# A hybrid encoder step on one core: the dense weight units in three places of a pair, each loaded where its remainder will be

## What is computed

```
xn  = rmsnorm(x);  z = xn @ w_in            # 1024 x 10248
br0 = (heads of an mLSTM over z) @ w_br_mlstm
br1 = (gated, spatially mixed z) @ w_br_gmlp
br2 = (attention of z into 256 memory tokens, k = mn @ w_mem_k, v = mn @ w_mem_v) @ w_br_mem
x   = x + (sum_b sigmoid(gate_b) * br_b) @ w_out
x   = x + hier_moe(rmsnorm(x))              # top-1 of 4 groups, top-2 of 8 experts in it
y   = rmsnorm_final(x)
```

## Time and profile before

| | us |
|---|---|
| median of 3 runs | 952.02 (951.14 to 954.7) |
| profiled execution, its own time | 952.92 |
| its span | 951.2 |
| PE busy | 883.6 (93%) |
| DVE busy | 608.0 (64%) |
| ACT busy | 473.1 (50%) |
| SP's queue moved | 171.46 MB of 182.92 MB in all |

### The profile page before, as it was taken

One profiled execution on the slowest core, in us unless ns is written; L12 is line 12 of the kernel. 1 busy time (PEld: TensorE's weight loads), 2 busy tenths in 40 slices (PEclk: granted clock), 3 DMA queues, 4 the chain that ended last, 5 costly groups with the idle time before them and its releaser, 6 DMA issues.

```text
span 951.2 us, 13084 instructions
## 1 busy us (share of the span) xinstructions
PE 883.6 (93%) x5274; PEld 788.7 (83%) x5274; DVE 608.0 (64%) x816; ACT 473.1 (50%) x572; POOL 46.2 (5%) x107
## 2 busy tenths in 40 slices
PE   2989999989999999989999999689999999999993
PEld 2958998979988999989999989478877777887871
DVE  4545367773244455476656545757888889898974
ACT  3554355553333134253333334656767767667652
POOL 5001101100010111000000000000000000000000
PEclk9999999999999999999999999779999999999996
DMA  8624642333446657735444465018999999999941
GB/s 256 186 90 133 221 144 90 111 101 111 136 116 96 132 148 111 171 96 185 135 133 134 155 203 218 0 33 320 352 347 361 350 336 348 350 345 354 350 176 58
DMA packets 99203, 182.92 MB, mean 192 GB/s; under 512 B 5368, under 2 KB 71120, under 8 KB 99136
## 3 DMA queue, kind: packets, MB, share of 16 engines
q1 hardware_dynamic: 95232, 171.46, 55.5%
q0 software_dynamic: 3072, 8.37, 3.5%
q10 hardware_dynamic: 832, 2.18, 0.9%
HBM read 176.17 MB, written 5.82 MB: 191 GB/s over the span
## 4 chain that ended last, share of the span: by engine, by line
PE 58%; DVE 7%; DMA 7%; ACT 3%; issue 3%; DVEq 0%; SPq 0%; ACTq 0%
PE pj L519 28%; PE pj L767 14%; PE pj L789 8%; DMA arena<-in_w_in 4%; DMA arena<-in_w_exp_down 3%; ACT unit_r L861 1%; PE ms L803 1%; DVE unit_r L1161 1%; ACT w_r L865 1%; PE ms L732 1%; DVE w_r L1170 1%; PE ms L652 1%; PE pj L732 1%; PE ms L777 1%; PE ms L676 1%
## 5 line engine op out<-in xcount | busy, mean ns | idle before, releaser
L1161 DVE TENSOR_TENSOR unit_r<-arena,unit_r 128x2048 fp32r<-128x2048 f32 x64 | 146.7, 2292 | 199.2 <-ACT unit_r L861 194.0
L1170 DVE TENSOR_TENSOR w_r<-arena,w_r 128x2048 fp32r<-128x2048 f32 x96 | 218.5, 2288 | 42.4 <-ACT w_r L865 41.7
L519 PE MATMUL pj<-xn_r,unit_r 128*128 128x320 f32 x1536 | 237.4, 314 | 3.4 <-DVE unit_r L1161 3.4
L519 PEld LDWEIGHTS pj<-xn_r,unit_r 128*128 128x128 f32 x1536 | 228.6, 190 | 7.9 <-issue 3.5
L865 ACT ACTIVATE w_r<-arena 128x2048 fp32r<-128x2048 f32 x96 | 183.4, 1916 | 39.5 <-DMA arena<-in_w_exp_up 26.9
L767 PE MATMUL pj<-w_r,xg 128*128 128x512 f32 x768 | 190.9, 398 | 0.0
L767 PEld LDWEIGHTS pj<-w_r,xg 128*128 128x128 f32 x768 | 141.9, 189 | 30.6
L861 ACT ACTIVATE unit_r<-arena 128x2048 fp32r<-128x2048 f32 x64 | 121.9, 1905 | 45.7 <-PE pj L519 22.8
L789 PE MATMUL pj<-w_r,hidT 128*128 128x512 f32 x384 | 93.2, 391 | 2.7 <-DVE w_r L1170 1.5
L789 PEld LDWEIGHTS pj<-w_r,hidT 128*128 128x128 f32 x384 | 71.6, 188 | 20.1 <-DVE w_r L1170 3.8
L519 PE MATMUL pj<-unit_r,xn_r 128*128 128x256 f32 (+1 forms) x576 | 70.0, 282 | 1.6 <-DVE unit_r L1161 1.6
(11 more groups left out here) (315 smaller groups left out, 741.6 us busy)
## 6 DMA issues: line engine op xcount, KB each, us to landing
arena<-in_w_in SPq DMA_DIRECT2D x40, 1024.0 KB, 5.2
arena<-in_w_exp_gate SPq DMA_DIRECT2D x64, 512.0 KB, 4.4
arena<-in_w_exp_up SPq DMA_DIRECT2D x64, 512.0 KB, 5.5
arena<-in_w_exp_down SPq DMA_DIRECT2D x64, 512.0 KB, 5.1
arena<-in_w_mem_k SPq DMA_DIRECT2D x4, 1024.0 KB, 9.4
arena<-in_w_mem_v SPq DMA_DIRECT2D x4, 1024.0 KB, 5.2
arena<-in_w_br_mem SPq DMA_DIRECT2D x4, 1024.0 KB, 7.9
arena<-in_w_br_mlstm SPq DMA_DIRECT2D x4, 1024.0 KB, 5.0
```

What stands on the lines that cost most here:

```text
L519: last = mm(bank_of(s)[0:out_rows, 0:out_cols], l, r, start=k == 0, stop=k == len(pairs) - 1)
L1161: v.tensor_tensor(unit_r[n % RING][:, 1, :], ringw[:, n % RING, :], unit_r[n % RING][:, 0, :], ALU.subtract).then_inc(u_lo, 1)
L1170: v.tensor_tensor(w_r[u % NS][:, 1, :], raw_w[u % NS], w_r[u % NS][:, 0, :], ALU.subtract).then_inc(m_lo, 1)
```

## The change

The six blocks of 2048 values become three places of a pair. A raw unit lands in the second half of its place. ACT writes the high part to the first half and DVE the remainder over the raw unit. Load n waits until PE has left unit n-3, instead of for the remainder of n-2. ACT's wait for PE ahead of a high part goes, because the load's own wait now covers it. The positions of both splits in the programs stay where they were, behind the last step of unit n-2 (the constant 2 instead of RING). As RING is 3, unit 2 is loaded ahead of x. The load of expert unit 4 waits until PE has left unit 62, the last one in the place that it overwrites.

```diff
-RING = 2
+RING = 3
...
-        RING0 = region(RING * UW)
-        ringw = at(RING0, RING, UW)
+        RING0 = region(2 * UW)
         SP0 = region(2 * 2 * UW)
-        unit_r = [rounded(f"unit_r{k}", SP0 + k * 2 * UW, 2, UW) for k in range(2)]
+        UNIT_AT = [(SP0, SP0 + 2 * UW, RING0)[(k - len(UNITS) + 1) % RING] for k in range(RING)]
+        unit_r = [rounded(f"unit_r{k}", o, 2, UW) for k, o in enumerate(UNIT_AT)]
+        ringw = [at(o + UW, UW) for o in UNIT_AT]
...
                 if n >= RING:
-                    sp.wait_ge(u_lo, n - RING + 1)
+                    sp.wait_ge(ready["pj"], _last_use[n - RING] + 1)
...
                     elif u == 4:
-                        sp.wait_ge(u_lo, len(UNITS))
+                        sp.wait_ge(ready["pj"], _last_use[len(UNITS) - 2] + 1)
...
             def unit_first_part(n):
                 act.wait_ge(unit_full[n % RING], 16 * (n // RING + 1))
-                if n >= RING:
-                    act.wait_ge(ready["pj"], _last_use[n - RING] + 1)
-                af(unit_r[n % RING][:, 0, :], ringw[:, n % RING, :], ACT.Copy).then_inc(u_hi, 1)
+                af(unit_r[n % RING][:, 0, :], ringw[n % RING], ACT.Copy).then_inc(u_hi, 1)
...
-                if s["ring"] == "pj" and s["last"] and s["unit"] + RING < len(UNITS):
-                    unit_first_part(s["unit"] + RING)
+                if s["ring"] == "pj" and s["last"] and s["unit"] + 2 < len(UNITS):
+                    unit_first_part(s["unit"] + 2)
...
-                v.tensor_tensor(unit_r[n % RING][:, 1, :], ringw[:, n % RING, :], unit_r[n % RING][:, 0, :], ALU.subtract).then_inc(u_lo, 1)
+                v.tensor_tensor(unit_r[n % RING][:, 1, :], ringw[n % RING], unit_r[n % RING][:, 0, :], ALU.subtract).then_inc(u_lo, 1)
...
-                if s["ring"] == "pj" and s["last"] and s["unit"] + RING < len(UNITS):
-                    unit_second_part(s["unit"] + RING)
+                if s["ring"] == "pj" and s["last"] and s["unit"] + 2 < len(UNITS):
+                    unit_second_part(s["unit"] + 2)
```

More of the change, by code:

```diff
@@ L466, in _ @@
                 if n >= RING:
-                    sp.wait_ge(u_lo, n - RING + 1)
+                    sp.wait_ge(ready["pj"], _last_use[n - RING] + 1)
                 src = I[name][0, :, col:col + 256].rearrange("(k p) n -> p k n", p=128)
-                sp.dma_start(ringw[:, n % RING, :].rearrange("p (k n) -> p k n", n=256), src).then_inc(unit_full[n % RING], 16)
+                sp.dma_start(ringw[n % RING].rearrange("p (k n) -> p k n", n=256), src).then_inc(unit_full[n % RING], 16)
             def load_unit(lv, u):
```

## The result

The changed kernel took 982.74 us (median of 4 runs, 977.43 to 985.99) where the kernel before took 953.36 beside it (951.14 to 955.05): a ratio of 1.0304, interval 1.0252 to 1.0357, 29.4 us more. On another chip, later, it was 972.98 against 947.18: 1.0284, interval 1.0224 to 1.0344.

A forecast was written before the change was run, and what follows sets the result against it. PE was taken as the bound, busy 883.6 us of 951.2. Costs of 3.6 + 2.0 + 2.4 + 2.8 = 10.8 took the profiled 952.92 to 963.7, less 0.9 to the runs' median: 962.8, range 950 to 972.

The forecast's parts named there:

- terms 1 and 3: Unit 29's load caught in the slow stretch, cost 3.6 us; expert burst delayed behind load 63, cost 2.4 us.
- (c): Rival: every landing moves with its issue and unit 29 lands like unit 30; 20.5 us more, 972.5; chance 0.12.
- the four terms: Costs at unit 29 (3.6 us), other caught loads (2.0), handover to the experts (2.4) and the clock (2.8).
- Start: Unit 2's load goes ahead of x, so x lands later; cost 0, at most 5.2 us if cover is gone.
- Unit 29: Out of memory attention: load issued behind state outputs lands at 302, deadline 298.35; cost 3.6 us, bounds 0 and 6.9.
- The other loads: Units 39, 32 and 36, near later state outputs: +1 us for 39, +1 for both others; bounds -6.4 and 11.4.
- Unit 39: Slowest load, starting 5.4 us later: cost 5.4, 0 or a gain depending on what sets its landing; +1 us taken.
- (b): Rival: load 39 lands earlier, PE's 5.0 us of remainder waits and one clock loss vanish; 949.4; chance 0.08.
- Handover: Dense stage to experts: load 63 and the expert burst behind it start 6.8 us later; cost 2.4 us, bounds 0 and 3.5.
- Clock: Half clock behind new idle times at unit 29 and the handover, 1.4 us each; cost 2.8 us, bounds 0 and 2.8.
- rest of the handover, experts: Expert unit 4 asked for at about 592 instead of 586, read after the gather at 639; cost 0.
- signs: ACT idle before unit 29, unit 39 landing at 396 plus PE's lateness, expert wait about 7 us, half clock for 3.4 us.

The follow-up runs named there:

- c1: The changed kernel with only the prompt's n output per head, the sample's left out (half the small writes): 949.46 us, ratio 1.0017.
- a2: The changed kernel without the outputs of the state n (eight DMAs of 256 single 4-byte values): 950.48 us, ratio 1.0032.
- a3: The changed kernel without the outputs of the state C (eight DMAs of 256 KB), n outputs kept: 977.05 us, ratio 1.0306.
- b3: The changed kernel, complete, with n transposed on PE and written by two DMAs in rows of 512 bytes: 950.18 us, ratio 1.0044.
- c2: The changed kernel, complete, each head's n outputs held until the high part of unit 29, 32, 36 or 39 is done: 957.48 us, ratio 1.0108.
- a1: The kernel before, layout unchanged, with load n also waiting until PE has left unit n-3: 977.24 us, ratio 1.0307.
- b1: The changed kernel with the first four expert units' loads put ahead of dense load 63 on SP's queue: 971.07 us, ratio 1.0232.
- b2: The kernel before, complete, with n written by two DMAs in rows of 512 bytes: 945.69 us, ratio 0.9981.
- d0: The changed kernel again, unaltered, on another chip: 972.98 us against 947.18, ratio 1.0284.

## Why the prediction was right or wrong

The prediction was 962.8, range 950 to 972; the time was 982.74. The sign, the mechanism and the places of terms 1 and 3 were right. The size was wrong by a factor of 2.7, and the time lies beyond the worst rival, (c) with 972.5. Even the upper bounds of the four terms, 6.9, 11.4, 3.5 and 2.8, make only 24.6 of the 29.4.

**Start: right.** Nothing was lost. PE was 0.7 ahead at unit 26, less than executions with the same start differ there (280.87 in c1, 284.14 in a2).

**Unit 29: right in kind, a little small.** I chose a landing at 302 and it was 303.6, inside the bounds. PE's start moved from 302.55 to 307.91, 5.4 us, where I had 3.6. The sentence of the Trainium skill on read-modify-write below 512 B ("DMA: Bandwidth & Descriptors", Specifications) fits what a3, c1 and b3 show: outputs of single 4-byte values make the stretch, and rows of 512 bytes don't. No run shows what the engines do with the small ones. The formula in the SWDGE section of that page of the Trainium skill is for transfers issued from GpSimd, and I applied it to a load on SyncE's queue, so the 5.2 of a quiet load and the 21.2 in the stretch are no test of it; my estimate of 4.4 us for this load was too low in either case.

**The other loads: this step failed.** I gave units 32 and 36 together 1 us, "but land with several microseconds in hand". They cost 9.4 and 11.0, with the clock. I judged their slack by how long they took before (12.0 and 12.7 us), and not by how long unit 30's took, 17.5, in the very place to which they were moving: 22.0 and 19.9 is what they then took. The row was in my list, and I had used it as a bound for unit 29 alone. Even rival (c), "every landing moves with its issue", moved the issue and kept the duration. Counted from the last n output, as at c2, the landing could have been had from rows of before: unit 30's came 23.7 us behind that output (281.46 to 305.20). The same behind 311.94 is 335.7, and 4.2 us of conversions make 339.9, where PE started on unit 32 at 332.46: 7.4 us of idle time, and 7.0 were measured. That PE was already late by 6.8 from unit 29 plays no part in it, since output, load and need all moved together.

One thing more was missing. I did write down that something stands behind a waiting DVE, but only for unit 29, where it was covered; at unit 36 it was L1314, and that is where PE stopped.

a1 and c1 show that this is the term: a1 has the same waits with the issue time alone changed, and c1, with 12.7 and 10.8 us in place of 22.0 and 19.9, has no wait at units 32 and 36.

**Unit 39.** The half of rival (b) came true: the load started later and took 15.6 us instead of 22.2. But PE's wait for it was only 1.6 and went to 0.4, so it brought 1.2 and not 5.0.

**Handover: right.** I had 2.4 for the idle time and 1.4 for the clock. Measured: 2.7 idle, and 4.5 with the clock. ACT's start on the first expert unit, given as 582.6, was this (the change, timeline of ACT):

```profile
607.41 1.92 ACT L864 ACTIVATE w_r<-arena 128x2048 fp32r<-128x2048 f32 x1 [13.59 <-DMA arena<-in_w_exp_up]
```

Less the 26.0 that PE was late by then it is 581.4. b1 took it away by the order on SP's queue alone, as the step says.

**Clock: one cause, sized wrong.** I had two dips of 1.4. There were three new ones in the middle and one at the end: 1.4, 2.6, 3.7 and 1.6 (13.05 us for 96 matmuls, where 22.91 for 192 make 11.5 for 96). I took the size from a dip of 3.4 us behind 2.2 us of idle time; behind idle times of 6.7 and 7.0 us it lasted 10.2, and PE worked in it for up to 7.7.

Summed as the prediction does it:

| term | predicted | measured |
|---|---|---|
| start | 0 | -0.7 |
| unit 29, idle | 3.6 | 6.1 |
| units 32, 36 and 39, idle | 2.0 | 12.9 |
| handover, idle | 2.4 | 2.7 |
| clock | 2.8 | 7.7 |
| rest of the handover, experts | 0 | 1.2 |
| sum | 10.8 | 29.9 |

The measured column is the table of late starts, with the clock losses taken out: 7.5 - 1.4 = 6.1; 9.4 + 11.0 - 1.2 - 2.6 - 3.7 = 12.9; at the handover 2.9, of which 2.7 are idle time. The fourth dip costs nothing in this sum, because this execution had no half clock in its first res steps (192 matmuls in 22.91 us) and the kernel before had the earlier trace rows; compared like with like the clock is 7.7 + 1.6.

What I named as signs came as said: ACT idle ahead of unit 29, the wait for the experts grown (13.6 us of idle time, not 7), PE idle in the res steps, and the half clock behind each, though 6.8 us long behind unit 29 where I had 3.4. The wait for unit 29 stands in the list as "issue".

## What to carry to other kernels

When a load is issued later, price it with the duration of a transfer in the place that it moves to, not with its own old one, and look there for what other queues do, however few the bytes: 2 KB of single values held the core's transfers at 28 to 41 GB/s for some 15 us. Where a slow stretch sets the landing, count it from what starts the stretch. If issues hang on the engine that is being delayed, ask what moves together with it: a stall that delays issue and need alike isn't won back, but it doesn't lengthen the next one either. A late load's cost can surface at an instruction that never reads it, so list what stands behind the waiting engine for each load and not just for the first; and a free tile that looks like more buffering gives less lead if the load must wait for it longer.

## What the runs showed of the hardware

Outputs of single 4-byte values slow transfers on another queue, for 22 to 33 ns a value (5.6 to 7.5 us for 256, 14.7 to 16.8 for 512, in c1 and the change), while the DMA engines are shown 59 to 82% busy at 28 to 41 GB/s; the same values in two outputs of 512-byte rows did not (5.0 us for the load 1.4 us behind them, b2). A high DMA share thus doesn't tell that much is moved. The granted clock stayed at half (1.2 GHz) for 3.4, 6.8 and 10.2 us behind idle times of 2.7, 5.9 and 7.0 us, in part while PE still stood still, and each microsecond of work in it cost 0.45 to 0.48. The length doesn't follow the idle time alone: in d0 4.7, 4.2 and 5.0 us of idle time had 6.8, 3.4 and 10.2 us of half clock. The dip isn't certain: behind the same 2.23 us of idle time ahead of the res steps it was there in the kernel before and in most runs (192 matmuls in 24.3 to 24.5 us), and it was not in the change's first profile (22.91) or in c2's (22.92). Why, no run here shows.
